# Opening of a hybrid decoder step: the sample rows held as 128 rows, two roots on GpSimd, block 0's weights between the token tiles

## The chip, the core and the metric

One NeuronCore of a Trainium2 chip runs the whole step. The metric is device time in microseconds, from the start of the execution to its end; lower is better. The engines are TensorE (PE), VectorE (DVE), ScalarE (ACT), GpSimd (POOL) and SyncE (SP), which only issues transfers; each runs its own instruction stream, and semaphores tie them together.

## The reference, cut to what matters

One layer over 512 prompt tokens and 8 sample tokens. The change touches only its first lines, the RMSNorm of the 520 token rows and what feeds the combined projection:

```python
def rmsnorm(x, g):
    xf = x.astype(jnp.float32)
    y = xf * lax.rsqrt(jnp.mean(xf * xf, -1, keepdims=True) + NORM_EPS)
    return (y * g.astype(jnp.float32)).astype(x.dtype)

def project(x, g_norm, w_in, pos):
    z = rmsnorm(x, g_norm) @ w_in          # w_in: 2048 x 8848
    q_r, k_r, v_r, g_r, q_a, k_a, v_a, g_a, q_i, k_i, w_i = jnp.split(z, offs, axis=-1)
    ...

hp, hs = x_prompt, x_sample                # (1, 512, 2048) and (8, 1, 2048)
```

Retention heads, an indexer with top-k selection, sparse attention, the output projection and a final norm follow; they are the same before and after.

## The kernel before

The tokens stand in five tiles of `XT`: four prompt tiles of 128 rows by 2048 columns (x0 to x3) and the sample tile, 8 rows by 2048 (index `QT`). They are taken in the order `ARRIVAL` = 0, 1, sample, 2, 3, and everything that is numbered by arrival (the column of `st4`, the semaphores `x_sq`, `x_norm`, `x_tr`) follows it.

Every tile goes through the same steps. ScalarE issues its load and squares it with a running sum (`squares`). VectorE makes the inverse root of the mean square (`norms`, which calls `rsqrt`, a shift and a subtraction on the bits and three Newton steps: 12 small linked instructions with the mean). VectorE multiplies the tile by its root and by the gain rows `gb` (`scale`). TensorE turns the tile into columns, 16 transposes of 128 by 128 in four groups, each group one PSUM bank (`turn_tokens`). ScalarE rounds a bank into the high part `Hh` (`high`), and VectorE subtracts that from the bank for the low part `Hl` (`low`), because every product with weights is made of three: high by high, low by high, high by low. The banks of the turns are 4 to 7 in rotation, so from the fifth group on a group waits for the `low` that frees its bank (`h_lo`).

The gain rows come from TensorE too: a product of a column of ones with the gain vector into banks 0 to 3, copied by VectorE into `gb`. `keep_busy` is a run of transposes whose result nobody reads.

The weights stream in 43 blocks through `Wraw`, two halves each. ScalarE rounds a half (`hi`), GpSimd makes the rest (`lo`, for block 0 the `W0l` and `W0h` instructions), and TensorE multiplies. Block 0 holds the index keys and index weights, 144 columns; its products are written out by hand. TensorE's order in the opening is: gain rows, filler, turns of x0 and x1, filler, index keys of tokens 0 to 255 over the first half of the rows of w_in, turns of the sample tile and of x2, index keys over the second half, turns of x3, index weights of tokens 128 to 255, and then, when every `low` is done, the late index products over tokens 256 to 519. From block 1 on the blocks follow one another.

SP's queue holds gains and identity, then waits until x2 has landed and issues block 0's two halves, the constants and the rest of the weights, each half when the buffer it goes into is free. VectorE's order is gain copies, root of x0 and x1 together, both scalings, root of the other three together, the `low` of x0 and x1, and then scaling and `low` in turns for the sample tile, x2 and x3.

Of the kernel before, what the change touches and what calls it, by code (L numbers as in the profile page):

```python
# [30 lines left out]
F32 = mybir.dt.float32  # L31
# [6 lines left out]
P = 128  # L38
# [39 lines left out]
def build(nc, x_prompt, x_sample, cache_k, cache_v, cache_kidx, state_ret, page_table, norm_g, w_in,  # L78
# [3 lines left out]
    with ctx:  # L82
# [3 lines left out]
        def sem(name):  # L86
            return ctx.enter_context(nc.semaphore(name))
# [51 lines left out]
        ptb, o = place("ptb", [P, NS, PAGES], I32, o)  # L139
        scores, o = place("scores", [NS * SEC, SKEY + 4], F32, 0)  # L140
# [88 lines left out]
        x_in = [sem(f"x_in{i}") for i in range(5)]  # L229
        x_sq = sem("x_sq"); st4_set = sem("st4_set"); g_tr = sem("g_tr"); g_row = sem("gain_row_in"); ones_set = sem("ones_set"); g_mm = sem("gain_rows_mm"); x_norm = sem("x_norm"); x_tr = sem("x_tr")  # L230
# [108 lines left out]
        def _(sp):  # L339
# [30 lines left out]
            sp.wait_ge(x_in[2], 16)  # L370
            weights(0, 0)
            weights(0, 1)
# [98 lines left out]
        def _(act):  # L471
# [93 lines left out]
            def squares(i, c):  # L565

                act.wait_ge(x_in[i], 16)
                r = rows(i)
                if i == QT:
                    act.wait_ge(st4_set, 1)  # L570
                if c:
                    act.wait_ge(x_sq, c)
                nc.scalar.activation(junk[0:r, :], XT[0:r, i, :], ACT.Square,
                                     accum_out=st4[0:r, c:c + 1]).then_inc(x_sq, 1)

            def high(pos, which=range(4)):

                i = ARRIVAL[pos]
                for g in which:
                    v = 4 * pos + g  # L580
                    act.wait_ge(x_tr, v + 1)
                    nc.scalar.activation(Hh[:, 4 * g:4 * g + 4, tok(i)], turned_tile(v, rows(i)),
                                         ACT.Copy).then_inc(h_hi, 1)

            for pos, i in enumerate(ARRIVAL):
                src = x_prompt[0, P * i:P * i + P, :] if i < QT else x_sample.rearrange("b o m -> (b o) m")
                act.dma_start(XT[0:rows(i), i, :], src).then_inc(x_in[i], 16)
            act.dma_start(ptb[:, :, :].rearrange("p b j -> p (b j)"),
                          page_table.rearrange("b j -> (b j)").partition_broadcast(P)).then_inc(s_ptab, 16)
            for c, i in enumerate(ARRIVAL):  # L590
                squares(i, c)
# [245 lines left out]
        def _(pool):  # L837
# [12 lines left out]

            pool.wait_ge(g_mm, 4)
# [124 lines left out]
        def _(dve):  # L976
            chain = [0]

            def link(ins):

                chain[0] += 1
                ins.then_inc(dch, 1)
                dve.wait_ge(dch, chain[0])
# [3 lines left out]
            def rsqrt(x, done=None):  # L987

                r, w = x.shape
                y, z = rsq[0:r, 0, 0:w], rsq[0:r, 1, 0:w]  # L990
                link(v_.tensor_scalar(y.bitcast(I32), x.bitcast(I32), 1, None, ALU.arith_shift_right))
                link(v_.tensor_scalar(y.bitcast(I32), y.bitcast(I32), -1.0, float(0x5f3759df), ALU.mult, ALU.add))
                for step in range(3):
                    link(v_.tensor_tensor(z, y, y, ALU.mult))
                    link(v_.scalar_tensor_tensor(z, z, -0.5, x, ALU.mult, ALU.mult))
                    ins = v_.scalar_tensor_tensor(y if step < 2 else x, z, 1.5, y, ALU.add, ALU.mult)
                    if done and step == 2:
                        ins.then_inc(done, 1)
# [4 lines left out]
            def norms(a, b):

                s = st4[:, a:b]
                dve.wait_ge(x_sq, b)
                link(v_.tensor_scalar(s, s, 1.0 / DM, EPS, ALU.mult, ALU.add))
                rsqrt(s)

            def column(i):  # L1010

                return ARRIVAL.index(i)

            def scale(i):
                r = rows(i)
                v_.scalar_tensor_tensor(XT[0:r, i, :], XT[0:r, i, :], st4[0:r, column(i):column(i) + 1], gb[0:r, :],  # L1016
                                        ALU.mult, ALU.mult).then_inc(x_norm, 1)

            def low(pos):

                i = ARRIVAL[pos]
                for g in range(4):
                    v = 4 * pos + g
                    dve.wait_ge(h_hi, v + 1)
                    v_.tensor_tensor(Hl[:, 4 * g:4 * g + 4, tok(i)], turned_tile(v, rows(i)),
                                     Hh[:, 4 * g:4 * g + 4, tok(i)].bitcast(F32), ALU.subtract).then_inc(h_lo, 1)

            v_.memset(ysq[:, :, :], 0.0)
            v_.memset(st4[:, 2:3], 1.0).then_inc(st4_set, 1)
# [22 lines left out]
            dve.wait_ge(h_lo, 20)  # L1052
# [376 lines left out]
        def _(pe):  # L1429
# [48 lines left out]
            def turn_tokens(pos):  # L1478

                i = ARRIVAL[pos]  # L1480
                r = rows(i)
                pe.wait_ge(x_norm, pos + 1)
                for g in range(4):
                    v = 4 * pos + g
                    if v >= 4:
                        pe.wait_ge(h_lo, v - 3)
# [31 lines left out]
            keep_busy(8, 3)  # L1518
# [417 lines left out]
```

## Time and profile before

| | us |
|---|---|
| median of three runs | 1217.83 |
| lowest and highest run | 1217.45, 1219.92 |
| the profiled execution's own time | 1220.82 |
| its span (first to last instruction) | 1219.0 |
| TensorE busy in the span | 1176.8 |
| VectorE busy | 620.0 |
| GpSimd busy | 570.6 |
| ScalarE busy | 452.1 |

The rows below come from this one execution; times in them are us from the start of the span. The profile's chain of waits follows the work that ended last back to its start, and its shares tell on which engine a delay reaches the end. In a timeline a row is one instruction or a run of equal ones, with the start, the time that it took, and in brackets how long its engine had stood idle and what ended that. Matmuls are pipelined: the time of one is longer than the distance to the next.

### The profile page before, as it was taken

What the parts mean: (1) busy time and instruction counts of PE and PEld (TensorE: products, weight loads), DVE (VectorE), ACT (ScalarE), POOL (GpSimd) and SP (SyncE); (2) the same over time, 40 slices, a digit from 0 to 9 for tenths busy, and PEclk for the clock granted to TensorE, in tenths of its full rate; (3) what the DMA queues carried; (4) which work ended last, traced back from release to release, by engine and by line L of the source; (5) the groups of instructions that cost most, each with busy time, mean ns of one, the idle gap of its engine ahead of it and who ended that gap; (6) DMA issues with size and microseconds to landing.
All of it is one profiled execution on the core that took longest, in us unless ns stands there. A gap on an engine that the chain in (4) does not pass through costs nothing.

```text
span 1219.0 us, 21955 instructions
## 1 busy us (share of the span) xinstructions
PE 1176.8 (97%) x9172; PEld 1110.3 (91%) x9172; DVE 620.0 (51%) x1199; ACT 452.1 (37%) x791; POOL 570.6 (47%) x262
## 2 busy tenths in 40 slices
PE   7999999899999999999999989999999999999995
PEld 5999995456999999999999979999999999999995
DVE  6500005998996994899998305343442544010013
ACT  5322225664223333333424323342524253232332
POOL 1355545240434333333635485846666384546450
PEclk9999999999999999999999999999999999999998
DMA  7233346380242222222343316446353525432213
GB/s 271 77 113 118 123 126 235 116 266 17 75 134 70 70 84 93 70 70 70 87 113 99 107 35 176 113 116 165 101 154 88 141 70 200 134 103 78 94 35 140
DMA packets 152840, 138.58 MB, mean 114 GB/s; under 512 B 4653, under 2 KB 145053, under 8 KB 151069
## 3 DMA queue, kind: packets, MB, share of 16 engines
q1 hardware_dynamic: 144502, 110.72, 30.5%
q0 software_dynamic: 6976, 22.03, 5.5%
q10 hardware_dynamic: 1280, 4.66, 1.0%
q8 instruction: 61, 1.00, 0.3%
q14 instruction: 21, 0.17, 0.0%
HBM read 127.02 MB, written 10.34 MB: 113 GB/s over the span
## 4 chain that ended last, share of the span: by engine, by line
PE 91%; DVE 4%; ACT 2%; issue 1%; DMA 1%; another core or an unknown queue 1%; DVEq 0%; ACTq 0%
PE bank L1448 25%; PE bank L1449 25%; PE bank L1450 25%; PE bank L1466 6%; PE bank L1559 2%; PE bank L1670 1%; PE bank L1652 1%; DVE bm L1083 1%; PE bank L1587 1%; DVE XT L1016 1%; PE bank L1825 1%; ACT mix L650 1%; DMA XT<-in_x_prompt 1%; PE bank L1596 1%
## 5 line engine op out<-in xcount | busy, mean ns | idle before, releaser
L1448 PE MATMUL bank<-Hh,Wh 128*128 128x264 f32 (+2 forms) x2432 | 711.8, 293 | 2.7 <-DVE Hl L1288 2.1
L1449 PE MATMUL bank<-Hl,Wh 128*128 128x264 f32 (+2 forms) x2432 | 703.4, 289 | 0.4 <-issue 0.4
L1450 PE MATMUL bank<-Hh,Wl 128*128 128x264 f32 (+2 forms) x2432 | 702.2, 289 | 0.5 <-issue 0.4
L842 POOL TENSOR_TENSOR Wl<-Wraw,Wh 128x2048 fp32r<-128x2048 f32 x84 | 386.8, 4606 | 477.3 <-ACT Wh L489 476.9
L1448 PEld LDWEIGHTS bank<-Hh,Wh 128*128 128x128 f32 x2432 | 459.7, 189 | 7.3 <-issue 6.4
L1449 PEld LDWEIGHTS bank<-Hl,Wh 128*128 128x128 f32 x2432 | 459.6, 189 | 3.1 <-issue 2.7
L1450 PEld LDWEIGHTS bank<-Hh,Wl 128*128 128x128 f32 x2432 | 458.7, 189 | 1.5 <-issue 1.5
L489 ACT ACTIVATE Wh<-Wraw 128x2048 fp32r<-128x2048 f32 x84 | 160.5, 1912 | 362.5 <-PE bank L1450 362.3
L1387 DVE TENSOR_TENSOR Y<-Y,bank 128x512 f32 (+1 forms) x16 | 10.4, 685 | 163.1 <-PE bank L1466 163.1
L1066 DVE COPY QS<-mix 128x128 f32<-128x128 f32 x1 | 0.3, 281 | 140.4 <-ACT mix L495 140.4
L870 POOL DMA_INDIRECT kx<-in_cache_kidx,pidx x32 | 30.4, 950 | 45.2 <-PE bank L1466 38.0
L1466 PEld LDWEIGHTS bank<-ident,kx 128*128 128x128 f32 x256 | 27.1, 141 | 23.8 <-issue 21.1
L900 POOL TENSOR_TENSOR XS<-XS,rot 128x520 f32<-128x520 f32 x16 | 21.2, 1322 | 44.6 <-ACT XW L547 44.6
L1466 PE MATMUL bank<-ident,kx 128*128 128x128 f32 x256 | 34.9, 279 | 7.0 <-ACT mix L650 4.7
L650 ACT ACTIVATE mix<-bank 128x512 f32<-128x512 f32 x64 | 34.9, 609 | 18.0 <-PE bank L1587 10.1
L1113 DVE MAX8 best<-scores 32x8 f32<-32x1025 f32 x32 | 38.9, 1217 | 5.1 <-ACT scores L677 4.1
L1145 DVE MAX8 top<-cand 8x8 f32<-8x1024 f32 x32 | 38.9, 1215 | 1.0
L1115 DVE FIND_INDEX8 besti<-best,scores 32x8 uint32<-32x1025 f32 x32 | 38.6, 1207 | 0.0
L1147 DVE FIND_INDEX8 besti<-top,cand 8x8 uint32<-8x1024 f32 x32 | 38.6, 1205 | 0.0
L1149 DVE MATCH_REPLACE8 cand<-top,cand 8x1024 f32<-8x1024 f32 x32 | 38.3, 1197 | 0.0
L1117 DVE MATCH_REPLACE8 scores<-best,scores 32x1025 f32<-32x1025 f32 x31 | 37.2, 1199 | 0.0
L1559 PE MATMUL bank<-kiT,mix 128*128 128x256 f32 (+2 forms) x96 | 33.8, 504 | 2.2 <-issue 1.4
(258 smaller groups left out, 1226.9 us busy)
## 6 DMA issues: line engine op xcount, KB each, us to landing
Wraw<-in_w_in SPq DMA_DIRECT2D x36, 1024.0 KB
Wraw<-in_w_in SPq DMA_DIRECT2D x64, 512.0 KB
Wraw<-in_w_out SPq DMA_DIRECT2D x16, 1024.0 KB
XT<-in_x_prompt ACTq DMA_DIRECT2D x4, 1024.0 KB, 9.0
sp__98<-in_state_ret SPq DMA_DIRECT2D x8, 512.0 KB, 4.0
out<-sp__98 SPq DMA_DIRECT2D x8, 512.0 KB, 5.1
Y<-in_x_prompt SPq DMA_DIRECT2D x1, 4096.0 KB
out<-Y SPq DMA_DIRECT2D x4, 1024.0 KB
```

Of the source, the lines that this page charges most:

```text
L489: nc.scalar.activation(Wh[:, a, :, :], Wraw[:, a, :, :], ACT.Copy).then_inc(w_hi, 1)
L650: nc.scalar.activation(kT[:, u % 6, :], bank[3 + u % 3][:, :], ACT.Copy).then_inc(kt_ev, 1)
L842: nc.gpsimd.tensor_tensor(Wl[:, a, :, :], Wraw[:, a, :, :], Wh[:, a, :, :].bitcast(F32), ALU.subtract).then_inc(w_lo, 1)
L1113: link(v_.max(top, row))
L1115: link(v_.max_index(besti[:, 8 * (k // 3):8 * (k // 3) + 8], top, row))
L1145: link(v_.max(top, cand[:, :]))
L1147: link(v_.max_index(besti[0:NS, 8 * (k // 3):8 * (k // 3) + 8], top, cand[:, :]))
L1448: mm(bank[i][:, 0:w], wh, Hh[:, kk, s], start=(a == 0 and k == 0), stop=False)
L1449: mm(bank[i][:, 0:w], wh, Hl[:, kk, s], start=False, stop=False)
L1450: last = mm(bank[i][:, 0:w], wl, Hh[:, kk, s], start=False, stop=(a == 1 and k == KC - 1))
L1466: return nc.tensor.transpose(out, in_, ident[0:k, 0:k])
L1559: mm(bank[4 + i % 4][:, 0:w], mix[:, h, tok(t)], kiT[:, 0:w], start=True, stop=True).then_inc(si_mm, 1)
```

## The change

The sample tile gets a buffer of its own, `xs0`: row (k, b) holds columns 128k to 128k + 127 of sample b, so 8 rows of 2048 become 128 rows of 128. Its gains come as `gs0` in the same shape, by a transfer of their own. Its square yields 128 partial sums; a matrix `same`, built from the identity, lets one product on TensorE (`sum_mm`) give every row the sum of its sample. One transpose turns the whole tile (in place of 16), with one `high` and one `low` (in place of four).

GpSimd makes the inverse roots of x0 and of x2 (`norm_root`, 14 linked instructions on one column each) ahead of its weight work. VectorE keeps the root of x1 and the sample together and that of x3 alone. In `rsqrt` the shift and the subtraction become one instruction, everywhere it is called.

Block 0's weights are issued by ScalarE between x2 and x3, and SP waits for x3 instead of x2 before the constants; the page table moves from ScalarE's queue to SP's. The turns use a table of banks, with banks 0 to 3 for x1, so that x1's turns wait for no `low`. The orders change: VectorE scales x0 before it makes the root of x1 and the sample, scales the sample before the first `low`, and makes the root of x3 after scaling x2; ScalarE squares x3 after the high part of the sample; TensorE does the index weights of tokens 128 to 255 before the turns of x3. The filler is split.

The core of the diff:

```diff
+        COLUMN = {0: 0, 1: 1, QT: 2, 2: 3, 3: 4}
+        GROUPS = {0: (0, 1, 2, 3), 1: (4, 5, 6, 7), QT: (8,), 2: (9, 10, 11, 12), 3: (13, 14, 15, 16)}
+        TURN_BANK = (4, 5, 6, 7, 0, 1, 2, 3, 4, 5, 6, 7, 4, 5, 6, 7, 4)
...
-            sp.wait_ge(x_in[2], 16)
-            weights(0, 0)
-            weights(0, 1)
+            sp.dma_start(gs0[:, :], norm_g[0].rearrange("(k c) -> k c", k=KT).unsqueeze(1).to_broadcast([KT, NS, P])
+                         ).then_inc(gs_in, 16)
+            sp.wait_ge(x_in[3], 16)
+            sp.dma_start(ptb[:, :, :].rearrange("p b j -> p (b j)"),
+                         page_table.rearrange("b j -> (b j)").partition_broadcast(P)).then_inc(s_ptab, 16)
...
-            for c, i in enumerate(ARRIVAL):
-                squares(i, c)
+            rows_in(0)
+            rows_in(1)
+            act.dma_start(xs0[:, :], x_sample[:, 0, :].rearrange("b (k c) -> k b c", k=KT)).then_inc(x_in[QT], 16)
+            rows_in(2)
+            first_weights(0)
+            first_weights(1)
+            rows_in(3)
+            squares(0, 0)
+            squares(1, 1)
+            squares(QT, 2)
+            squares(2, 3)
             high(0)
             hi(0, 0)
             hi(0, 1)
             high(1)
+            high(QT)
+            squares(3, 4)
             high(2)
             high(3)
-            high(4)
...
+            def norm_root(a, b):
+
+                x, y, z = st4[:, a:b], xs2[:, 1:2], xs2[:, 2:3]
+                g_ = nc.gpsimd
+                link(g_.tensor_scalar(x, x, 1.0 / DM, EPS, ALU.mult, ALU.add))
+                link(g_.tensor_scalar(y.bitcast(I32), x.bitcast(I32), -0.5, float(0x5f3759df), ALU.mult, ALU.add))
+                for step in range(3):
+                    link(g_.tensor_tensor(z, y, y, ALU.mult))
+                    link(g_.tensor_tensor(z, z, x, ALU.mult))
+                    link(g_.tensor_scalar(z, z, -0.5, 1.5, ALU.mult, ALU.add))
+                    ins = g_.tensor_tensor(y if step < 2 else x, z, y, ALU.mult)
+                    if step < 2:
+                        link(ins)
+                ins.then_inc(rstd, 1)
+
+            pool.wait_ge(x_sq, 1)
+            norm_root(0, 1)
+            pool.wait_ge(x_sq, 4)
+            norm_root(3, 4)
...
-                link(v_.tensor_scalar(y.bitcast(I32), x.bitcast(I32), 1, None, ALU.arith_shift_right))
-                link(v_.tensor_scalar(y.bitcast(I32), y.bitcast(I32), -1.0, float(0x5f3759df), ALU.mult, ALU.add))
+                link(v_.tensor_scalar(y.bitcast(I32), x.bitcast(I32), -0.5, float(0x5f3759df), ALU.mult, ALU.add))
...
+            dve.wait_ge(s_ident, 16)
+            link(v_.tensor_reduce(same8[:, :], ident[:, :].rearrange("p (k b) -> p b k", k=KT), AXX, ALU.add))
+            v_.tensor_copy(same[:, :, :], same8[:, :].unsqueeze(1).to_broadcast([P, KT, NS])).then_inc(same_ready, 1)
             for i in range(4):
                 dve.wait_ge(g_mm, i + 1)
-                link(v_.tensor_copy(gb[:, 512 * i:512 * i + 512], bank[i][:, :]))
+                v_.tensor_copy(gb[:, 512 * i:512 * i + 512], bank[i][:, :]).then_inc(gb_copied, 1)
             dve.wait_ge(g_tr, 1)
             link(v_.tensor_copy(gains_T[:, :], bank[7][:, 0:KT + NH]))
-            norms(0, 2)
-            scale(0)
-            scale(1)
-            norms(2, 5)
+            dve.wait_ge(gb_copied, 4)
+            scale(0, 1)
+            dve.wait_ge(x_sq, 2)
+            v_.tensor_scalar(st4[:, 1:2], st4[:, 1:2], 1.0 / DM, EPS, ALU.mult, ALU.add)
+            dve.wait_ge(sum_mm, 1)
+            link(v_.tensor_scalar(st4[:, 2:3], bank[3][:, 0:1], 1.0 / DM, EPS, ALU.mult, ALU.add))
+            rsqrt(st4[:, 1:3])
+            scale(1, 0)
+            dve.wait_ge(gs_in, 16)
+            scale(QT, 0)
             low(0)
             low(1)
-            scale(QT)
-            scale(2)
+            low(QT)
+            scale(2, 2)
+            dve.wait_ge(x_sq, 5)
+            link(v_.tensor_scalar(st4[:, 4:5], st4[:, 4:5], 1.0 / DM, EPS, ALU.mult, ALU.add))
+            rsqrt(st4[:, 4:5])
+            scale(3, 0)
             low(2)
-            scale(3)
             low(3)
-            low(4)
...
-            keep_busy(24, 6)
-            turn_tokens(0)
-            turn_tokens(1)
+            keep_busy(16, 6)
+            pe.wait_ge(same_ready, 1)
+            pe.wait_ge(x_sq, 3)
+            pe.wait_ge(gb_copied, 4)
+            mm(bank[3][:, 0:1], same[:, :, :].rearrange("p k b -> p (k b)"), xs2[:, 0:1], start=True, stop=True).then_inc(sum_mm, 1)
+            keep_busy(8, 6)
+            turn_tokens(0, 1)
+            keep_busy(8, 2)
+            turn_tokens(1, 2)
+            turn_tokens(QT, 3)
...
-            keep_busy(8, 3)
             pe.wait_ge(h_lo, 8)
             pe.wait_ge(w_lo, 1)
             index_keys(0, slice(0, CUT))
-            turn_tokens(2)
-            turn_tokens(3)
+            turn_tokens(2, 4)
             pe.wait_ge(w_lo, 2)
             index_keys(1, slice(0, CUT)).then_inc(acc_done, 1)
-            turn_tokens(4)
             index_weights(slice(P, CUT))
-            pe.wait_ge(h_lo, 20)
+            turn_tokens(3, 5)
+            pe.wait_ge(h_lo, 17)
```

Two engines' rows show the new orders. A row names the line, the operation, what it writes and reads, and the semaphores that it waits for. First ScalarE's opening, before (`x_in0` to `x_in4` are the landed tiles, `x_in4` the sample's, `x_sq` the squares done, `x_tr` the groups turned, `w_landed` the halves of block 0's weights):

```order
L587 DMA XT<-in_x_prompt 128x2048 x2
L587 DMA XT<-in_x_sample 8x2048
L587 DMA XT<-in_x_prompt 128x2048 x2
L588 DMA ptb<-in_page_table 128x256
L573 ACT_TABLE_LOAD
L573 ACTIVATE junk,st<-XT 128x2048 [waits x_in0]
L573 ACTIVATE junk,st<-XT 128x2048 [waits x_sq,x_in1]
L573 ACTIVATE junk,st<-XT 8x2048 [waits x_sq,st4_set,x_in4]
L573 ACTIVATE junk,st<-XT 128x2048 [waits x_sq,x_in2]
L573 ACTIVATE junk,st<-XT 128x2048 [waits x_sq,x_in3]
L582 ACTIVATE Hh<-bank 128x4x128 [waits x_tr] x4
```

and the same engine after:

```order
L602 DMA XT<-in_x_prompt 128x2048 x2
L610 DMA xs_53<-in_x_sample 128x1x128
L602 DMA XT<-in_x_prompt 128x2048
L606 DMA Wraw<-in_w_in 128x8x144 x2
L602 DMA XT<-in_x_prompt 128x2048
L591 ACT_TABLE_LOAD
L591 ACTIVATE junk,st<-XT 128x2048 [waits x_in0]
L591 ACTIVATE junk,st<-XT 128x2048 [waits x_sq,x_in1]
L589 ACTIVATE junk,xs_57<-xs_53 128x128 [waits x_sq,x_in4]
L591 ACTIVATE junk,st<-XT 128x2048 [waits x_sq,x_in2]
L598 ACTIVATE Hh<-bank 128x4x128 [waits x_tr] x4
```

Seven issues stand ahead of the table load where six stood, two of them weights, and the square of x3 has left the group of squares.

VectorE after the root of its second group, before (`Hl` is written by `low`, `XT` by `scale`, `h_hi` counts the high parts):

```order
L996 SCALAR_TENSOR_TENSOR st<-rsq 128x3 [waits dve_chain]
L1025 TENSOR_TENSOR Hl<-bank,Hh 128x4x128 [waits h_hi,dve_chain]
L1025 TENSOR_TENSOR Hl<-bank,Hh 128x4x128 [waits h_hi] x7
L1016 SCALAR_TENSOR_TENSOR XT<-XT,st,gb 8x2048
L1016 SCALAR_TENSOR_TENSOR XT<-XT,st,gb 128x2048
L1025 TENSOR_TENSOR Hl<-bank,Hh 128x4x8 [waits h_hi] x4
```

and after, from the end of the root of x1 and the sample:

```order
L1049 SCALAR_TENSOR_TENSOR st<-rsq 128x2 [waits dve_chain]
L1064 SCALAR_TENSOR_TENSOR XT<-XT,st,gb 128x2048 [waits dve_chain]
L1061 SCALAR_TENSOR_TENSOR xs_53<-xs_53,st,gs_54 128x128 [waits sample_gains_in]
L1071 TENSOR_TENSOR Hl<-bank,Hh 128x4x128 [waits h_hi] x8
L1071 TENSOR_TENSOR Hl<-bank,Hh 128x16x8 [waits h_hi]
L1064 SCALAR_TENSOR_TENSOR XT<-XT,st,gb 128x2048 [waits rstd_ready]
```

The root now stands between the scalings of x0 and x1, the sample's scaling has moved ahead of the eight `low`, and the scaling of x2 waits for GpSimd's second root.

## Rows read from the trace of the kernel before

**Rows 1.** The page's head, and its chain of waits by engine, shares of the span.

```profile
span 1219.0 us, 21955 instructions
...
PE 91%; DVE 4%; ACT 2%; issue 1%; DMA 1%; another core or an unknown queue 1%; DVEq 0%; ACTq 0%
```

**Rows 2.** Timeline of ScalarE and SyncE's queue: start, duration, engine, line, operation [idle before].

```profile
3.25 0.48 ACTq L588 DMA_DIRECT2D ptb<-in_page_table  x1
...
3.76 1.28 ACT L573 ACT_TABLE_LOAD   x1 [3.76 <-issue]
...
5.83 1.91 ACT L573 ACTIVATE junk<-XT 128x2048 f32<-128x2048 f32 x1 [0.78 <-DMA XT<-in_x_prompt]
...
9.35 1.91 ACT L573 ACTIVATE junk<-XT 128x2048 f32<-128x2048 f32 x1 [1.52 <-DMA XT<-in_x_prompt]
...
12.23 1.02 SPq L357 DMA_DIRECT2D Wraw<-in_w_in  x2
...
13.30 1.72 SPq L373 DMA_DIRECT2D rot<-in_c_rot  x1
```

**Rows 3.** Transfer issues of the first 60 us: count, KB, us to landing.

```profile
ident<-in_c_ident SPq DMA_DIRECT2D x1, 64.0 KB, 7.5
```

**Rows 4.** Timeline of VectorE, opening and tail.

```profile
9.94 0.69 DVE L1034 COPY gb<-bank 128x512 f32<-128x512 f32 x1 [1.02 <-PE bank L1471]
...
11.46 0.17 DVE L1007 TENSOR_SCALAR st<-st 128x2 f32<-128x2 f32 x1 [0.61 <-ACT junk L573]
...
13.83 4.62 DVE L1016 SCALAR_TENSOR_TENSOR XT<-XT,st,gb 128x2048 f32<-128x2048 f32 x2
...
20.73 3.28 DVE L1025 TENSOR_TENSOR Hl<-bank,Hh 128x512 fp32r<-128x512 f32 x5
...
26.35 4.59 DVE L1016 SCALAR_TENSOR_TENSOR XT<-XT,st,gb 8x2048 f32<-8x2048 f32 x2
...
37.10 2.48 DVE L1025 TENSOR_TENSOR Hl<-bank,Hh 128x512 fp32r<-128x512 f32 x4 [1.11 <-ACT Hh L582]
...
1207.20 0.17 DVE L991 TENSOR_SCALAR rsq<-st 128x3 int32<-128x3 int32 x1
```

**Rows 5.** Timeline of TensorE, opening.

```profile
16.24 1.97 PE L1466 MATMUL bank<-ident,XT 128*128 128x128 f32 x16 [1.07 <-DVE XT L1016]
...
21.57 3.50 PE L1466 MATMUL bank<-ident,XT 128*128 128x128 f32 x16 [3.37 <-DVE Hl L1025]
...
26.49 0.38 PE L1504 MATMUL bank<-Hh,W0h 128*128 128x256 f32 x1 [0.55 <-DVE Hl L1025]
...
31.19 1.94 PE L1466 MATMUL bank<-ident,XT 128*128 128x128 f32 x16 [0.52 <-DVE Hl L1025]
...
32.89 0.36 PE L1504 MATMUL bank<-Hh,W0h 128*128 128x256 f32 x1
...
35.83 1.91 PE L1466 MATMUL bank<-ident,XT 128*128 128x128 f32 x16
...
37.49 0.30 PE L1514 MATMUL bank<-Hh,W0h 128*32 128x128 f32 x1
...
39.64 0.39 PE L1504 MATMUL bank<-Hh,W0h 128*128 128x264 f32 x1
```

**Rows 6.** GpSimd: timeline, one group (mean ns); VectorE beside it at 990 us.

```profile
20.82 2.38 POOL L855 TENSOR_TENSOR W0l<-Wraw,W0h 128x1024 fp32r<-128x1024 f32 x1 [20.36 <-ACT W0h L484]
...
L918 POOL TENSOR_TENSOR QZ<-XS,XW 128x8 f32<-128x8 f32 x8 | 1.7, 212 | 0.0
...
990.56 4.63 POOL L842 TENSOR_TENSOR Wl<-Wraw,Wh 128x2048 fp32r<-128x2048 f32 x1 [1.48 <-ACT Wh L489]
...
992.70 8.12 DVE L1283 TENSOR_TENSOR Hl<-mix,Hh 128x512 fp32r<-128x512 f32 x4 [14.92 <-ACT Hh L731]
```

**Rows 7.** Busy us by window: PE, PEld, DVE, ACT, POOL, then granted clock, DMA.

```profile
21.00:22.00 1.00, 0.43 (x2) 0.46 (x3) 1.00 (x3) 0.72 (x1) 1.00 (x1) 0.69 0.00 0
...
22.00:23.00 1.00, 1.00 (x7) 1.00 (x6) 1.00 (x3) 0.30 (x1) 1.00 (x1) 0.50 0.00 0
```

More of the change, by code:

```diff
@@ L139, in build @@
         ptb, o = place("ptb", [P, NS, PAGES], I32, o)
+        xs0, o = place("xs0", [P, P], F32, o)
+        gs0, o = place("gs0", [P, P], F32, o)
+        same, o = place("same", [P, KT, NS], F32, o)
+        same8, o = place("same8", [P, NS], F32, o)
+        xs2, o = place("xs2", [P, 3], F32, o)
         scores, o = place("scores", [NS * SEC, SKEY + 4], F32, 0)
@@ L567, in squares @@
                 act.wait_ge(x_in[i], 16)
-                r = rows(i)
-                if i == QT:
-                    act.wait_ge(st4_set, 1)
                 if c:
                     act.wait_ge(x_sq, c)
[L573 to L580, printed above, removed]
-                    act.wait_ge(x_tr, v + 1)
-                    nc.scalar.activation(Hh[:, 4 * g:4 * g + 4, tok(i)], turned_tile(v, rows(i)),
-                                         ACT.Copy).then_inc(h_hi, 1)
@@ L585, in _ @@
[L585 to L589, printed above, removed]
-            for c, i in enumerate(ARRIVAL):
-                squares(i, c)
+                if i == QT:
+                    nc.scalar.activation(junk[:, 0:P], xs0[:, :], ACT.Square, accum_out=xs2[:, 0:1]).then_inc(x_sq, 1)
+                else:
+                    nc.scalar.activation(junk[:, :], XT[:, i, :], ACT.Square,
+                                         accum_out=st4[:, c:c + 1]).then_inc(x_sq, 1)
@@ new lines, in high, with rows_in, first_weights @@
+            def high(i):
+                for g, v in enumerate(GROUPS[i]):
+                    act.wait_ge(x_tr, v + 1)
+                    nc.scalar.activation(h_tile(Hh, i, g), turned_tile(v), ACT.Copy).then_inc(h_hi, 1)
+            def rows_in(i):
+                act.dma_start(XT[:, i, :], x_prompt[0, P * i:P * i + P, :]).then_inc(x_in[i], 16)
+            def first_weights(a):
+                act.dma_start(Wraw[:, a, :, 0:144], wiv[:, KC * a:KC * a + KC, 8704:8848]).then_inc(w_in_sem[a], 16)
@@ L849, in lo_loop, with link @@
                     lo(n, 1, step=step)
+            chain = [0]
+            def link(ins):
+                chain[0] += 1
+                ins.then_inc(nch, 1)
+                pool.wait_ge(nch, chain[0])
+            def norm_root(a, b):
[15 more added lines that the diff above has]
+            norm_root(3, 4)
             pool.wait_ge(g_mm, 4)
@@ L1000, in rsqrt, with scale @@
                         link(ins)
[L1003 to L1016, printed above, removed]
+            def scale(i, done):
+                if done:
+                    dve.wait_ge(rstd, done)
+                if i == QT:
+                    v_.scalar_tensor_tensor(xs0[:, :], xs0[:, :], st4[:, 2:3], gs0[:, :], ALU.mult, ALU.mult).then_inc(x_norm, 1)
+                    return
+                c = COLUMN[i]
+                v_.scalar_tensor_tensor(XT[:, i, :], XT[:, i, :], st4[:, c:c + 1], gb[:, :],
@@ L1017, in scale, with low @@
                                         ALU.mult, ALU.mult).then_inc(x_norm, 1)
[L1019 to L1023, printed above, removed]
+            def low(i):
+                for g, v in enumerate(GROUPS[i]):
                     dve.wait_ge(h_hi, v + 1)
-                    v_.tensor_tensor(Hl[:, 4 * g:4 * g + 4, tok(i)], turned_tile(v, rows(i)),
-                                     Hh[:, 4 * g:4 * g + 4, tok(i)].bitcast(F32), ALU.subtract).then_inc(h_lo, 1)
+                    v_.tensor_tensor(h_tile(Hl, i, g), turned_tile(v), h_tile(Hh, i, g).bitcast(F32),
+                                     ALU.subtract).then_inc(h_lo, 1)
@@ L1028, in _ @@
             v_.memset(ysq[:, :, :], 0.0)
-            v_.memset(st4[:, 2:3], 1.0).then_inc(st4_set, 1)
             v_.memset(ones[:, :], 1.0).then_inc(ones_set, 1)
+            dve.wait_ge(s_ident, 16)
+            link(v_.tensor_reduce(same8[:, :], ident[:, :].rearrange("p (k b) -> p b k", k=KT), AXX, ALU.add))
+            v_.tensor_copy(same[:, :, :], same8[:, :].unsqueeze(1).to_broadcast([P, KT, NS])).then_inc(same_ready, 1)
             for i in range(4):
                 dve.wait_ge(g_mm, i + 1)
-                link(v_.tensor_copy(gb[:, 512 * i:512 * i + 512], bank[i][:, :]))
+                v_.tensor_copy(gb[:, 512 * i:512 * i + 512], bank[i][:, :]).then_inc(gb_copied, 1)
@@ L1050, in _ @@
             dve.wait_ge(s_const, 80)
             dve.wait_ge(s_ptab, 16)
-            dve.wait_ge(h_lo, 20)
+            dve.wait_ge(h_lo, 17)
             link(v_.tensor_tensor(ptm[:, :, :], ptb[:, :, :].rearrange("p b (s j) -> p (b s) j", s=SEC),
@@ L1477, in _, with turn_tokens @@
             pe.wait_ge(s_ident, 16)
[L1478 to L1486, printed above, removed]
+            def turn_tokens(i, done):
+                pe.wait_ge(x_norm, done)
+                if i == QT:
+                    pe.wait_ge(h_lo, 1)
+                    turn(bank[TURN_BANK[8]][:, 0:P], xs0[:, :]).then_inc(x_tr, 1)
+                    return
+                for g, v in enumerate(GROUPS[i]):
+                    if v >= 9:
+                        pe.wait_ge(h_lo, 9 if v == 12 else v - 7 if v < 12 else v - 3)
                     for k in range(4):
                         c = P * (4 * g + k)
-                        last = turn(bank[4 + v % 4][:, P * k:P * k + r], XT[0:r, i, c:c + P], r)
+                        last = turn(bank[TURN_BANK[v]][:, P * k:P * k + P], XT[:, i, c:c + P])
                     last.then_inc(x_tr, 1)
```

9 lines of the change are left out of this document (7 added, 2 removed).

## The prediction

> **What bounds the kernel now.** The page's chain of waits comes first: 91% of the span lies on TensorE [rows 1], in weight products that follow one another. A change of the opening can therefore only move the moment at which that stream begins, and whatever it moves there is carried to the end unchanged. So I read the timeline of the first 50 us, engine by engine, and look at who waits for whom. TensorE's last real wait before the stream is for the split token tiles: the late index products begin at 39.64 [rows 5], 0.06 us after VectorE's last `low` ends (37.10 + 2.48 = 39.58 [rows 4]), and from there block 0 and block 1 run without a hole. VectorE works almost without pause from 11.46 to 36: root, two scalings, root, eight `low`, two more scalings [rows 4]. TensorE starts the index keys at 26.49, released by VectorE [rows 5], and needs 13.15 us from there to 39.64, nearly all of it busy. So there are two sections to price: VectorE's chain up to the eighth `low`, and TensorE's chain after it.
>
> **Section one, up to the eighth low (before: 26.44).**
>
> ScalarE. Its queue now issues seven loads, not six, and two of them are block 0's weights (1.02 us for the pair on SP, [rows 2]); the page table leaves it (0.48). The fourth prompt tile, x3, is issued behind the weight pair. The one issue behind such a pair in the trace, `rot`, took 1.72 us where the others take 0.35 to 0.6 [rows 2]. Taking 1.72 for x3, 1.25 more than usual, the table load moves from 3.76 to 5.55 and the first square from 5.83 to 6.83. If the issue does not stall, the square stays at 5.83, since x0's landing releases it [rows 2]; the upper bound is a rival below. Landing order costs nothing: the weights come behind x2 (here at 12.2, when SP was released), are used at about 18, and x3 is now squared only after the sample tile's high part, around 22.
>
> GpSimd. Root 0 is 14 linked instructions on one column. GpSimd's shortest arithmetic of the trace, 128x8, takes 0.21 us [rows 6]; with a link's gap of 0.04 (VectorE's 12 links take 11.46 to 13.83, 0.197 each for instructions of 0.16 [rows 4]) that is 14 x 0.25 = 3.5. A square needs 2.1 from its start to the reader's (9.35 to 11.46), so root 0 stands at 6.83 + 2.1 + 3.5 = 12.4; with no stall 11.4, with 0.3 a link 13.1.
>
> VectorE's gain rows. It now waits for the identity first, which lands 7.5 us after its issue, at 8.7 [rows 3], then makes `same` (two instructions, 0.3 each at most) and four gain copies of 0.69: 12.0. That is 1.4 later than before, and it is a floor under the first scaling however fast GpSimd is. So the first scaling starts at 12.45, not 13.83: **-1.4** (from -1.8 to -0.7).
>
> Between the two scalings stand two small scalars and ten links, 2.37 us, the same as the root that stood after them: 0. The sample scaling shrinks from 2.29 (half of the pair at 26.35 [rows 4]) to about 0.3 but moves ahead of the `low`s, **+0.3**; its gain of 2 us falls behind them. The eight `low` now have eight banks and run at 0.66 each (3.28 for five), 5.4 instead of 5.7 (20.73 to 26.44): **-0.3**.
>
> The shared port. Where VectorE and GpSimd both read SBUF, one stands still: a group of VectorE's subtractions with both inputs in SBUF began at 992.70, took 8.12 us for four that need 0.69 each, and the first got through only as GpSimd's 4.63 us subtraction from 990.56 ended [rows 6]. GpSimd's second root starts when the square of x2 is done, about 14.3, so it runs against VectorE's own root. If each of 12 VectorE instructions waits out one GpSimd instruction, that is 12 x 0.21 = 2.5; if it never waits, 0. GpSimd's hold is shorter than its 0.21 us, and I take **+1.0**. That root's last links are then held behind the second scaling (18.1 to 20.4) and the weight split W0l, 2.38 us a half [rows 6], begins at about 21 instead of 20.82: in time for TensorE.
> The Trainium skill, "SBUF — State Buffer", section "Who interferes with whom", speaks against this part of the change: it says that a VectorE instruction with two SBUF inputs and a GpSimd instruction that reads SBUF exclude each other for a whole instruction. By that rule the root costs up to the 2.5 above and the scalings, too, stop GpSimd; without it the sum would be 1.0 lower. The subtraction at 992.70 agrees; no row shows a scaling of this shape against GpSimd.
>
> Eighth low: 26.44 - 1.4 + 0.3 - 0.3 + 1.0 = about 26.1, and the index keys start at 26.2 instead of 26.49.
>
> **Section two, TensorE from there.** One half of the index keys takes 35.83 - 32.89 = 2.94, a tile's turns 32.89 - 31.19 = 1.7, the index weights 39.64 - 37.49 = 2.15 [rows 5]. Before, the sample turns and a wait lay between the index keys and tile 2 (tile 2 started at 31.19, 4.7 after the index keys). Now tile 2 follows at once, 26.2 + 2.95 = 29.15; the third scaling ends at about 28.8 and is covered. But the index weights now stand ahead of tile 3's turns, where before they covered the high and low parts of tile 3. From the first turn of a last tile to its last `low` are 39.58 - 35.83 = 3.75 us, of which only the turns were exposed. So the end is 29.15 + 1.7 + 2.94 + 2.15 + 3.75 = 39.7 against 39.64: **+0.05**. What the sample tile gives, this order takes back. VectorE is just in time for it (root and fourth scaling end near 33.8, `low` of tile 2 at 36.4, tile 3's turns at 35.9 need only its first group).
>
> The clock. TensorE's granted clock was 0.69 in 21 to 22 and 0.50 in 22 to 23 [rows 7], the 1.2 GHz level, after the engine had stood from 18.2 to 21.57; there VectorE covered the slow turns. After the change the filler turns ahead of the index keys are gone and TensorE stands from about 22.7 to 26.2 there, as long as it stood in the trace. If the clock falls, the index keys, which nothing covers, run at half rate: 2.94 us can lose up to about 1.7 (16 turns took 3.50 at that level and 1.97 above it [rows 5]). If not, 0. I take **+0.8**.
>
> The tail. Every VectorE root loses one of twelve links; only the one at 1207.2 [rows 4] is on the end's chain: **-0.2**. The others lie beside weight products.
>
> Moved at no cost: SP's constants start when x3 lands (about 18.5), take some 6 us of issue and delay block 1's weights by about 1 us; they are wanted only at 38.4. Their cover is 9 us. The page table is wanted by VectorE after its last `low`.
>
> **Sum:** 26.2 - 26.49 = -0.3 in section one; section two, +0.35 longer, brings it to +0.05; with the clock +0.8 and the tail -0.2 it is +0.65. The profiled execution, 1220.82 us (span 1219.0 [rows 1]), would take 1221.5. It lay 3.0 above the median of the three runs, so the forecast is 1217.83 + 0.65 = **1218.5 us**, no difference that can be told: a measurement of this kernel tells about 0.2%, 2.4 us, from nothing (the three runs themselves span 2.5).
>
> **Rivals.**
> *The roots are free.* ScalarE's issue does not stall (-0.4 left of it, by the floor of 12.0), the port costs nothing (-1.0) and the clock holds (-0.8): 1218.5 - 2.2 = 1216.3. For it: the first square has 0.8 us of slack in waiting for x0. Against it: the row at 992.70. It needs all three. Chance 0.15, and only with luck in the measurement over 0.2% faster.
> *The port in full.* VectorE's root and GpSimd's take turns link by link (+1.5 on what I took) and the clock falls for the whole of the index keys (+0.9); or, if GpSimd's root is quick and done before the second scaling ends, W0l goes first and the sample scaling waits out 2.38 us. Either way about +2.4: 1220.9. Chance 0.22; over 0.2% slower in two thirds of it.
> *ScalarE blocked by its own queue, slower.* x3's issue waits not 1.7 us but until the weights' many short rows, which stand behind 3 MB of tiles on the same queue, have begun to drain. x2 lands at 12.2; ScalarE would issue until then, load its table at 12.5 and square at 13.8 instead of 6.83. All of section one hangs on that square: +7, 1225.5. For it: `rot` did stall behind the same pair with an almost empty queue ahead. Against it: six loads of 4 MB were issued in the trace without a stall. It decides against the change from an issue of about 3.5 us on. Chance 0.14.
> *The forecast*, 0.49.
>
> **Numbers.** The range runs from 1215.9, the free roots less 0.4 for the spread of runs, to 1222.4, the full port with 1.5 for both of its forms together; what is left out is the blocked queue and some 0.05. Faster by over 0.2%: 0.06 (a third of the free roots). Slower: 0.14 + 0.15 + 0.05 from the forecast's upper edge = 0.34. Same: 0.60.
>
> **What would show it.** First square at 6.8, not 5.8 and not beyond 9; x3's issue near 1.7 us. GpSimd's root links at 0.25 us, the first scaling at 12.0 to 12.7. VectorE's root between the scalings longer than 2.4 us. GpSimd's W0l starting after the second scaling. Index keys at 26.2, and the granted clock in that stretch. TensorE standing for about 1.5 us ahead of the late index products, near 39.7. It is wrong if the late index products begin before 38 or after 42, or if anything behind them takes another time than now.

## The result, and the profile after

| | us |
|---|---|
| before, median of nine runs | 1217.83 |
| after, median of nine runs (lowest, highest) | 1222.73 (1221.16, 1226.9) |
| ratio after to before, 95% interval | 1.0036, 1.0025 to 1.0046 |
| the profiled execution of after, own time and span | 1221.33, 1219.5 |

The changed kernel is slower by 0.36%, some 4.4 us (3.0 to 5.6 by the interval). The forecast was no difference, 1218.5 us, in a range up to 1222.4. The median lies 0.3 us above that range; the ratio, turned into us (1222.2), lies 0.2 below its end. The sign that the prediction had named for being wrong did come: the late index products start after 42.

The two profiled executions differ by only 0.5 us, because that of before ran 3.0 us above its median and that of after 1.4 below. So the profiles are compared at one mark, the start of the late index products, behind which the kernels do the same work but for one instruction less in each root: 39.64 before [rows 5], 44.67 after, **+5.03 us**. Behind the mark the nine profiles of this study scatter: from the mark to the end of the span that of before took 1219.0 - 39.64 = 1179.4 us, that of after 1174.8, and all nine lie between 1174.2 and 1180.7. The scatter goes with the mean granted clock of the execution: 0.994 in after, 0.990 in before, 0.986 in the slowest behind the mark (e3 below, 1180.7). What is worth a few us behind the mark is therefore read from the timed runs alone. One execution of e7 below, 1644.59 us at a granted clock of 0.655, stays out of its ratio.

The page's chain of waits, answering [rows 1], has lost three points on TensorE, mainly to VectorE and GpSimd:

```profile
PE 88%; DVE 5%; ACT 2%; POOL 2%; issue 1%; ACTq 1%; another core or an unknown queue 0%; DVEq 0%; POOLq 0%
```

ScalarE of the changed kernel, queue and engine (start, us, engine, line, operation, [idle before]):

```profile
2.38 0.65 ACTq L602 DMA_DIRECT2D XT<-in_x_prompt  x1
3.06 4.20 ACTq L606 DMA_DIRECT2D Wraw<-in_w_in  x2
7.29 4.38 ACTq L602 DMA_DIRECT2D XT<-in_x_prompt  x1
11.70 1.28 ACT L591 ACT_TABLE_LOAD   x1 [11.70 <-issue]
12.99 1.91 ACT L591 ACTIVATE junk<-XT 128x2048 f32<-128x2048 f32 x1
...
15.09 1.91 ACT L591 ACTIVATE junk<-XT 128x2048 f32<-128x2048 f32 x1
```

These answer [rows 2]. Issuing block 0's two weight loads took 4.20 us (0.47 for the first of them, 3.70 for the second) and issuing x3 behind them 4.38; the table load stands at 11.70 where it stood at 3.76, and its bracket names "issue": no data was waited for. The first square is at 12.99, right behind the table load, where it was at 5.83.

VectorE of the changed kernel, answering [rows 4]:

```profile
7.66 0.38 DVE L1078 TENSOR_REDUCE same<-ident 128x8 f32<-128x128 f32 x1 [6.60 <-DMA ident<-in_c_ident]
...
8.21 2.55 DVE L1082 COPY gb<-bank 128x512 f32<-128x512 f32 x4
...
18.99 2.35 DVE L1064 SCALAR_TENSOR_TENSOR XT<-XT,st,gb 128x2048 f32<-128x2048 f32 x1 [8.13 <-POOL st L896]
...
23.51 2.35 DVE L1064 SCALAR_TENSOR_TENSOR XT<-XT,st,gb 128x2048 f32<-128x2048 f32 x1
25.78 0.34 DVE L1061 SCALAR_TENSOR_TENSOR xs<-xs,st,gs 128x128 f32<-128x128 f32 x1
26.04 5.06 DVE L1071 TENSOR_TENSOR Hl<-bank,Hh 128x512 fp32r<-128x512 f32 x9
31.03 3.22 DVE L1064 SCALAR_TENSOR_TENSOR XT<-XT,st,gb 128x2048 f32<-128x2048 f32 x1
```

VectorE, which worked almost without pause from 11.46 on before, now stands for 8.13 us and waits for GpSimd's root; that root waits for ScalarE's square (14.63 in GpSimd's bracket below). The stall of the queue goes through three engines to the first scaling.

TensorE and GpSimd of the changed kernel, answering [rows 5, 6]:

```profile
30.96 0.39 PE L1568 MATMUL bank<-Hh,W0h 128*128 128x256 f32 x1 [2.54 <-DVE Hl L1071]
...
38.95 0.22 PE L1578 MATMUL bank<-Hh,W0h 128*32 128x128 f32 x1
...
40.86 1.92 PE L1522 MATMUL bank<-ident,XT 128*128 128x128 f32 x16
44.67 0.39 PE L1568 MATMUL bank<-Hh,W0h 128*128 128x264 f32 x1 [1.89 <-DVE Hl L1071]
...
1204.75 0.88 PE L1522 MATMUL bank<-ident,mix 128*128 128x128 f32 x6 [0.48 <-ACT mix L579]
```

```profile
15.09 0.19 POOL L890 TENSOR_SCALAR st<-st 128x1 f32<-128x1 f32 x1 [14.63 <-ACT junk L591]
...
18.66 0.19 POOL L896 TENSOR_TENSOR st<-xs 128x1 f32<-128x1 f32 x1
...
19.77 1.62 POOL L890 TENSOR_SCALAR st<-st 128x1 f32<-128x1 f32 x1 [0.92 <-ACT junk L591]
...
23.70 2.21 POOL L896 TENSOR_TENSOR xs<-xs 128x1 f32<-128x1 f32 x1
...
29.29 0.47 POOL L910 TENSOR_TENSOR W0h<-Wraw,W0h 128x128 fp32r<-128x128 f32 x1
29.69 2.41 POOL L909 TENSOR_TENSOR W0l<-Wraw,W0h 128x1024 fp32r<-128x1024 f32 x1
32.04 2.52 POOL L910 TENSOR_TENSOR W0h<-Wraw,W0h 128x128 fp32r<-128x128 f32 x1
```

The index keys start at 30.96 (26.49 before) and the late products 13.71 us later; before it was 13.15. TensorE stands 1.89 us ahead of the late products, which it did not do before. The granted clock was 1.00 over the index keys. On GpSimd a small instruction of the root takes 0.19 us, unless a scaling of VectorE runs: then 1.62 and 2.21. The small weight instruction W0h takes 0.47, and beside the third scaling 2.52.

### The profile page after: what moved, and what is told of

It reads as the page before. It is cut to its first block, busy times and chain, and to the rows that moved or that the text cites. A ratio compares the mean times of both kernels' runs of the same rounds, so it can differ in the third digit from the quotient of the medians.

```text
span 1219.5 us, 21936 instructions
## 1 busy us (share of the span) xinstructions
PE 1174.9 (96%) x9159; PEld 1107.8 (91%) x9159; DVE 617.0 (51%) x1185; ACT 449.4 (37%) x788; POOL 580.8 (48%) x290
## 3 DMA queue, kind: packets, MB, share of 16 engines
q10 hardware_dynamic: 3344, 5.71, 1.3%
## 4 chain that ended last, share of the span: by engine, by line
PE 88%; DVE 5%; ACT 2%; POOL 2%; issue 1%; ACTq 1%; another core or an unknown queue 0%; DVEq 0%; POOLq 0%
PE bank L1504 24%; PE bank L1505 24%; PE bank L1506 24%; PE bank L1522 5%; PE bank L1621 2%; PE bank L1732 1%; PE bank L1714 1%; PE bank L1649 1%; DVE bm L1139 1%; ACT mix L678 1%; PE bank L1887 1%; DVE XT L1064 1%; DVE Hl L1071 1%; PE bank L1658 1%; POOL rowf L948 1%
```

## The experiments

Theory: ScalarE is held in its own queue by the weight loads, and that alone makes the kernel slower; the rest of the change gives something. Rivals: GpSimd's roots and the SBUF port cost it; the order of the index weights costs it; the clock does. All kernels are set against the kernel before on the same chip; a ratio is turned into us with 1217.83.

| kernel | first square | index keys | late products, against 39.64 | ratio, 95% interval | us |
|---|---|---|---|---|---|
| after | 12.99 | 30.96 | +5.03 | 1.0036, 1.0025 to 1.0046 | +4.4 |
| e1_w0_on_sp | 5.80 | 23.84 | -1.02 | 0.9991, 0.9981 to 1.0001 | -1.1 |
| e2_w0_sp_keys_last | 5.79 | 23.75 | -3.11 | 0.9972, 0.9961 to 0.9982 | -3.4 |
| e3_before_w0_on_act | 14.04 | 32.58 | +7.04 | 1.0068, 1.0054 to 1.0083 | +8.3 |
| e4_w0_first | 9.72 | 27.69 | +2.84 | 1.0019, 1.0010 to 1.0029 | +2.3 |
| e5_keys_last_filler | 5.66 | 23.61 | -3.51 | 0.9970, 0.9958 to 0.9982 | -3.7 |
| e6_vector_roots | 5.66 | 27.52 | +0.95 | 0.9993, 0.9984 to 1.0002 | -0.9 |
| e7_w0_on_sp_filler | 5.77 | 23.77 | -2.16 | 0.9986, 0.9977 to 0.9995 | -1.7 |

Column four comes from one profiled execution, the last from the timed runs; they agree within 1.3 us but for e6, which is told below. In e1 and e6 the interval reaches 1, so these two can't be told from before.

**e1: the weights back on SP.**

```diff
             rows_in(2)
-            first_weights(0)
-            first_weights(1)
             rows_in(3)
...
+            sp.wait_ge(x_in[2], 16)
+            weights(0, 0)
+            weights(0, 1)
             sp.wait_ge(x_in[3], 16)
```

> The changed kernel with block 0's two weight loads given back to SP, behind x2's landing; ScalarE issues x3 right behind x2. Theory (ScalarE was blocked issuing): table load near 3.8 and first square near 5.8 instead of 11.70 and 12.99. GpSimd's root then ends near 11.7 (3.76 us from the second square's start, as measured), the first scaling starts near 11.8, the index keys 12.0 later as in the changed kernel, near 23.8, and the late index products 13.7 behind those, near 37.5 (changed kernel 44.67, before 39.64). Time 1222.73 - 7.2 = 1215.5 us. Rival (GpSimd's roots and the SBUF port are what costs): late products stay beyond 42 and the time at 1220 or more.

Timelines of e1's queues and ScalarE, then TensorE:

```profile
2.37 1.17 ACTq L605 DMA_DIRECT2D XT<-in_x_prompt  x2
3.56 1.28 ACT L594 ACT_TABLE_LOAD   x1 [3.56 <-issue]
5.80 1.91 ACT L594 ACTIVATE junk<-XT 128x2048 f32<-128x2048 f32 x1 [0.95 <-DMA XT<-in_x_prompt]
...
11.83 1.03 SPq L373 DMA_DIRECT2D Wraw<-in_w_in  x2
```

```profile
23.84 0.39 PE L1569 MATMUL bank<-Hh,W0h 128*128 128x256 f32 x1 [2.97 <-DVE Hl L1072]
...
28.31 1.91 PE L1523 MATMUL bank<-ident,XT 128*128 128x128 f32 x16
...
38.62 0.39 PE L1569 MATMUL bank<-Hh,W0h 128*128 128x264 f32 x1 [1.90 <-DVE Hl L1072]
```

The first square is back at 5.80 and again waits for x0's landing; the first scaling starts at 11.86, the index keys at 23.84, both as expected, with GpSimd's roots and the port as they were. So these are not what costs; the rival falls. Nor is it x3's later landing (SP, which waits for it, goes on at 17.90 in after and at 14.40 in e1): x3 is squared only at 29.78 in after. The late products came at 38.62 and not at 37.5, and the time, by the ratio, at 1216.7 and not at 1215.5: the first half of the index keys took 28.31 - 23.84 = 4.47 us. Windows of e1 (length, then busy us of PE, PEld, DVE, ACT, POOL, then the granted clock, DMA share, GB/s):

```profile
23.00:24.00 1.00, 0.16 (x1) 0.17 (x2) 1.00 (x4) 0.60 (x2) 1.00 (x1) 1.00 0.33 34
...
25.00:26.00 1.00, 1.00 (x6) 1.00 (x6) 1.00 (x1) 0.00 (x0) 1.00 (x1) 0.50 1.09 387
```

The granted clock was 0.50, the 1.2 GHz level, in 25 to 27, after TensorE had stood for 2.97 us and had begun to work again. e7 tests that.

**e3: the kernel before with this one edit.**

```diff
-            weights(0, 0)
-            weights(0, 1)
...
                 act.dma_start(XT[0:rows(i), i, :], src).then_inc(x_in[i], 16)
+                if i == 2:
+                    for a in range(2):
+                        act.dma_start(Wraw[:, a, :, 0:144], wiv[:, KC * a:KC * a + KC, 8704:8848]).then_inc(w_in_sem[a], 16)
```

> The kernel before with one edit: block 0's two weight loads are issued by ScalarE between x2 and x3, not by SP when x2 has landed. Theory (ScalarE's issue is blocked by these loads): the pair takes about 4.2 us to issue, x3 about 4.4, table load near 12.1 and first square near 13.4, +7.6 against before; VectorE's first root, which waits for two squares, starts near 17.6 instead of 11.46, +6.2. Time 1217.9 + 6.2 = 1224. Rival (the other parts of the change cost it): first square within 1 us of 5.83 and 1218.

```profile
2.67 4.56 ACTq L588 DMA_DIRECT2D Wraw<-in_w_in  x2
7.26 4.97 ACTq L585 DMA_DIRECT2D XT<-in_x_prompt  x1
...
14.04 1.91 ACT L571 ACTIVATE junk<-XT 128x2048 f32<-128x2048 f32 x1
```

```profile
18.25 0.17 DVE L1008 TENSOR_SCALAR st<-st 128x2 f32<-128x2 f32 x1 [7.25 <-ACT junk L571]
```

ScalarE's and VectorE's timelines of e3 show the same two long issues without anything else of the change. The time is 8.3 us worse (6.6 to 10.1), 6.2 were expected; VectorE's first root starts at 18.25 where it started at 11.46, +6.8, and the late products at 46.68, +7.04. The edit is enough to make a kernel slower, by more than the whole change did.

**e4: the weights first of all in ScalarE's queue.**

```diff
+            first_weights(0)
+            first_weights(1)
             rows_in(0)
...
             rows_in(2)
-            first_weights(0)
-            first_weights(1)
```

> The changed kernel with block 0's two weight loads issued by ScalarE first of all, ahead of x0, so that no backlog stands before them. Theory A (the engine is held because short rows are queued behind tiles that have not drained): the pair issues in about 1.0 us and x0 in about 1.7, the table load comes near 6 to 7, and the first square waits only for x0, which stands behind 1.15 MB more (2.9 us at the 390 GB/s of that stretch), near 8.8; late products near 40.5, time 1218.5. Theory B (that many short rows hold the engine wherever they stand): issues of 8 us again, table load near 11.7, time 1222.7 or more.

```profile
0.76 1.08 ACTq L606 DMA_DIRECT2D Wraw<-in_w_in  x2
1.87 1.96 ACTq L602 DMA_DIRECT2D XT<-in_x_prompt  x2
...
5.65 1.28 ACT L591 ACT_TABLE_LOAD   x1 [5.65 <-issue]
9.72 1.91 ACT L591 ACTIVATE junk<-XT 128x2048 f32<-128x2048 f32 x1 [2.78 <-DMA XT<-in_x_prompt]
```

With nothing queued ahead the same pair issues in 1.08 us, not 4.20, and the two tiles behind it in 1.96. Theory A holds: the short rows hold the engine only with a backlog ahead of them. Long rows alone didn't hold it either (six loads before the change), so it takes both. SP's queue isn't in the way: in after it issues nothing between 3.2 and 17.90. What it is ahead in the queue that holds the engine, the rows or the bytes, isn't shown.
The square now waits for x0, whose bytes stand behind the weights (9.72; 8.8 was expected). The late products came at 42.48, not at 40.5: 0.9 us of that is the square, and some 1.1 the granted clock, which was 0.50 from 29 to 31, so that the first half of the index keys took 32.17 - 27.69 = 4.48 us. The kernel ends 2.3 us above before (1.2 to 3.5).
The Trainium skill ("Perfetto Trace Analysis", section "What 'DMA-bound' means") reads the rows of an issuing queue as descriptor generation. The two loads are the same in after and in e4, and their issue took 4.20 and 1.08; so here most of the long row is waiting, and the measured rows decide.

**e2: with the weights on SP, the index weights behind the turns of x3 again.**

```diff
-            index_weights(slice(P, CUT))
             turn_tokens(3, 5)
+            index_weights(slice(P, CUT))
```

> As e1_w0_on_sp, and the index weights stand behind the turns of x3 again. In the changed kernel TensorE stood 1.89 us ahead of the late products; the index weights (1.92 us) can cover that, but VectorE's low parts of x2 and x3 follow one another without a gap from the fourth scaling's end, and bound it. Expected: late products 0.7 us earlier than in e1_w0_on_sp, near 36.8, time 1214.8. Rival (the order decides alone, VectorE has room): 1.9 us earlier, 1213.6. If TensorE's order means nothing: equal to e1_w0_on_sp.

VectorE, then TensorE of e2:

```profile
29.33 2.35 DVE L1065 SCALAR_TENSOR_TENSOR XT<-XT,st,gb 128x2048 f32<-128x2048 f32 x1
31.60 4.86 DVE L1072 TENSOR_TENSOR Hl<-bank,Hh 128x512 fp32r<-128x512 f32 x8
```

```profile
32.43 2.36 PE L1523 MATMUL bank<-ident,XT 128*128 128x128 f32 x16 [0.27 <-DVE Hl L1072]
...
36.53 0.37 PE L1569 MATMUL bank<-Hh,W0h 128*128 128x264 f32 x1
```

The late products start at 36.53 (36.8 expected), right after the eight `low` end at 36.46. TensorE no longer stands ahead of them: the index weights fill that place, and the turns of x3 are paced by the `low`s (2.36 us, with a wait of 0.27 for one), so VectorE bounds. The kernel is faster than after and than before, by 0.28% (0.18 to 0.39%).

**e5 and e7: sixteen filler turns ahead of the index keys, in e2 and in e1.**

```diff
+            pe.wait_ge(h_lo, 4)
+            keep_busy(16, 7)
             pe.wait_ge(h_lo, 8)
```

> e2_w0_sp_keys_last with sixteen filler turns ahead of the index keys (TensorE waits there for the first four low parts, then turns the identity into a spare bank), as the kernel before had eight at that place. In the profile of e2 the granted clock stayed at 1.00 over the index keys, in that of e1 it fell to 0.50 in 25 to 27. Clock theory: some executions of e2 lose it too, so the median falls by 0 to 0.7 us against e2 (ratio to before 0.9966 to 0.9972); late products near 36.5 in the profile, as in e2. Rival (the filler stands in the way of the index keys): index keys later than 24.0 and the time 0.5 us or more above e2.

> e1_w0_on_sp with the same sixteen filler turns ahead of the index keys. If e1's shortfall (late products 38.62 where 37.5 was expected) is the clock, which fell to 0.50 in the middle of the index keys there: granted clock 1.00 from 23 to 28, the index keys take 2.8 instead of 4.5 us, late products near 37.5, time 1.1 us below e1 (ratio to before 0.9982). If not: late products at 38.6 and the time of e1.

In e7 the first half of the index keys and what stands before x2's turns ran from 23.77 to 27.12 at a granted clock of 1.00, and the late products started at 37.48 (37.5 expected); the ratio moved by 0.0005 of the 0.0009 expected, less than the intervals can tell. In the same profile the clock fell elsewhere, behind the mark, after TensorE had stood for 1.90 us ahead of the late products:

```profile
37.00:38.00 1.00, 0.52 (x4) 0.53 (x5) 0.85 (x2) 1.00 (x1) 0.00 (x0) 1.00 0.00 0
...
39.00:40.00 1.00, 1.00 (x7) 1.00 (x6) 1.00 (x1) 1.00 (x2) 1.00 (x1) 0.50 0.00 0
```

e5 has neither of the two stands. Its index keys start at 23.61 at 1.00, so the filler is not in the way, but its time (0.9970) can't be told from e2's (0.9972): what the filler is worth there isn't shown. What the order of the index weights is worth shows between e7 and e5: 1.35 us at the late products, 1.9 by the ratios.

**e6: e2 without GpSimd's roots.**

```diff
-            pool.wait_ge(x_sq, 1)
-            norm_root(0, 1)
-            pool.wait_ge(x_sq, 4)
-            norm_root(3, 4)
...
+            dve.wait_ge(x_sq, 1)
+            link(v_.tensor_scalar(st4[:, 0:1], st4[:, 0:1], 1.0 / DM, EPS, ALU.mult, ALU.add))
+            rsqrt(st4[:, 0:1])
...
-            scale(2, 2)
             dve.wait_ge(x_sq, 5)
+            link(v_.tensor_scalar(st4[:, 3:5], st4[:, 3:5], 1.0 / DM, EPS, ALU.mult, ALU.add))
+            rsqrt(st4[:, 3:5])
+            scale(2, 0)
             scale(3, 0)
```

> e2_w0_sp_keys_last with the two GpSimd roots undone: VectorE makes x0's root ahead of the gain copies and one root for x2 and x3 together ahead of the third scaling. By the rows: first scaling 12.95 instead of 11.79, index keys 24.9 instead of 23.75; third scaling ends at 30.0 instead of 27.2, since the joint root waits for x3's square; late products 38.5 instead of 36.53, time 2.0 us above e2 (ratio to before 0.9988). Rival (GpSimd's roots cost more than they give, by the SBUF port): late products at 36.5 or earlier and a time equal to e2 or below it.

VectorE, then GpSimd of e6:

```profile
13.47 2.35 DVE L1061 SCALAR_TENSOR_TENSOR XT<-XT,st,gb 128x2048 f32<-128x2048 f32 x1
...
20.22 2.46 DVE L1058 SCALAR_TENSOR_TENSOR xs<-xs,st,gs 128x128 f32<-128x128 f32 x1
22.60 5.06 DVE L1068 TENSOR_TENSOR Hl<-bank,Hh 128x512 fp32r<-128x512 f32 x9
```

```profile
19.83 2.70 POOL L906 TENSOR_TENSOR W0l<-Wraw,W0h 128x1024 fp32r<-128x1024 f32 x1 [19.37 <-ACT W0h L505]
```

The rival falls: taking GpSimd's roots away makes e2 slower by 2.6 us (0.9993 against 0.9972), where 2.0 were expected. And the port shows itself: the sample scaling, 0.35 us elsewhere, took 2.46, since W0l had begun 0.4 us before it. The index keys of this profile start at 27.52, 2.6 us behind the 24.9 expected: 2.1 is that hold, and 0.5 the first scaling, which came at 13.47 and not at 12.95. The late products stand at 40.59, 2.1 behind the 38.5 expected. The timed runs can't hold all of it (2.6 us against e2, where the mark shows 4.06); the two instructions start within 0.4 us of each other, and in how many executions W0l comes first isn't shown.

## Why the prediction failed, step by step

**ScalarE's issue: the step that failed.** "Taking 1.72 for x3": that row, `rot` behind the pair, was read with a queue that had drained, while here three tiles, 3 MB together, stood ahead. Measured: 4.20 for the pair, for which the forecast took 1.02, and 4.38 for x3. The forecast put the first square at 6.83; it came at 12.99. The rival "ScalarE blocked by its own queue" described it nearly to the row (table load at 12.5, square at 13.8; measured 11.70 and 12.99), and its price of 7 us is what the index keys show between after and e1: 30.96 - 23.84 = 7.12. What held its chance at 0.14, "six loads of 4 MB were issued in the trace without a stall", said nothing on short rows: these were loads of few long ones. ScalarE's queue carried 1280 packets for 4.66 MB before and 3344 for 5.71 MB after.

**The rest of the change: sized too dear.** Without the stall it is worth -1.1 us (e1, whose interval reaches 0) to -1.7 (e7), not +0.65. The index keys stand at 23.84, not at 26.2:
- First scaling 11.86 in e1, not 12.45. The gain copies were done at 10.76 in after, since VectorE had the identity at 7.66 and not 8.7; the floor of 12.0 was not there. GpSimd's root took 3.76 (15.09 to 18.85 in after), 3.5 were taken.
- Between the scalings and for the sample scaling: 4.52 us from the first scaling's start to the second's in after, against 2.31 + 2.37 counted; the sample scaling 0.34 against 0.3. Right.
- The `low`s: from the first of them to the index keys 4.92 us in after (26.04 to 30.96), and 5.4 were counted for eight. None of them waits there; nine take 5.06.
- The port: +1.0 was taken. VectorE's root links kept their pace: the root between the scalings took 2.25 us in e1 (14.13 to 16.38), with GpSimd's root beside it, and 2.21 in e6 (15.74 to 17.95), without. What the port did was to hold GpSimd behind scalings (2.21, 2.52), and VectorE's third scaling behind W0l (3.22 instead of 2.35), where in after the index keys covered all but 0.24 us of it. The Trainium skill ("SBUF — State Buffer", section "Who interferes with whom") has the port held for a whole instruction by whoever came first; the 2.21 and the 2.46 of e6 agree. Small instructions that alternate cost 0.04 us in all, not 1.0.

**Section two: right.** 13.5 us without the clock were counted from index keys to late products; 13.71 in after and in e7. That the index weights' new place takes back what the sample tile gives was right too: putting them back gave 1.35 to 1.9 us.

**The clock.** +0.8 was taken, between 0 and 1.7. Over the index keys the granted clock was 1.00 in after, which cost nothing, and 0.50 for two us in e1, which cost 1.1: both lie within what was allowed for, and which of them comes differs between these executions.

**The tail.** -0.2 was counted; from TensorE's last row to the end of the span it is 1219.0 - 1204.03 = 14.97 before and 1219.5 - 1204.75 = 14.75 after. The row of before:

```profile
1204.03 0.88 PE L1466 MATMUL bank<-ident,mix 128*128 128x128 f32 x6 [0.61 <-ACT mix L561]
```

**How it fits together.** The rivals were taken as alternatives. In fact "the roots are free" (1216.3, by e1 and e7 1216.1 to 1216.7) and "ScalarE blocked" (+7) both happened, and 7 less 1.5 is 5.5; the mark shows 5.03, which lies inside the interval of the timed runs (3.0 to 5.6). That the time still fell at the upper end of the range is luck: the stall, which the range left out, was partly made up by terms that had been sized too dear, and the end itself had been set by the port, which cost next to nothing in after.

## What to carry to other kernels

An issue row's length holds for that place in that queue (1.08 and 4.20 us for the same pair): before a load of many short rows is put on a compute engine's queue, look at what will still be draining ahead of it, and at what that engine has to do next; where there is a queue whose engine has nothing else to do, as SP here (e1), it belongs there. Price rivals that don't exclude each other together as well as one by one. When work is moved ahead of a last tile's turns, ask what it used to cover there.

## What the runs showed of the hardware

- The same two loads of 576 KB took 1.08 us to issue on ScalarE with nothing ahead (e4), 1.02 to 1.38 on SP once x2 had landed, and 4.20 (after) and 4.56 (e3) behind three prompt tiles, nearly all of it in the second load; a following tile of 1 MB then took 4.38 and 4.97, where a tile with no weights ahead took 0.36 to 0.65.
- GpSimd's linked one-column instructions repeat every 0.275 us (0.19 of it busy), VectorE's every 0.19 to 0.20; side by side, VectorE's whole root took 0.04 us more (2.25 in e1, 2.21 in e6) and GpSimd's links stood at 0.28 (e1).
- A VectorE scaling with two SBUF inputs stretched a 0.19 us GpSimd instruction to 2.21, and W0l on GpSimd a 0.35 us scaling to 2.46.
- The same stand of 2.97 us on TensorE was followed by a fall to the 1.2 GHz level in e1 and e4 and by none in e2.
- The record of the granted clock need not show a slow stretch: in after, once TensorE had stood for 4.00 us, the 16 turns of x0 took 3.67 us, as long as at the 1.2 GHz level before (3.50), while the record says 1.00. No `low` waited for them there.

```profile
21.39 3.67 PE L1522 MATMUL bank<-ident,XT 128*128 128x128 f32 x16 [1.34 <-DVE XT L1064]
```

```profile
22.00:23.00 1.00, 1.00 (x7) 1.00 (x6) 0.83 (x6) 0.45 (x1) 0.73 (x4) 1.00 0.78 235
```
